# Hymba-style decoder on one core: attention logits two heads at a time, gate rows by a block diagonal, and a new place for three low parts of the output weights

## The chip, the cores and the metric

The program runs on one core of one Trainium2 chip. The metric is the device time of one execution in microseconds (us). Shorter is better. The names of the engines are those of the profile: PE does matrix products (PEld loads its weights), DVE is the vector engine, ACT the scalar engine, POOL is GpSimd, SP only issues DMAs.

## What is computed

The reference is a decoder of two layers over 1024 tokens of width 1024. Each layer projects the normed input once, gives the parts to three mixers, maps their outputs by one output projection, and adds a SwiGLU feed-forward block:

```python
h = rms_norm(x, norm_w[0])
proj = h @ w_in
(mq, mk, mv, mo, mi, mf, aq, ak, av, iq, ik, iw, sz, sxbc, sdt) = jnp.split(proj, _split_points(), axis=-1)
hm = mlstm_chunkwise(...)        # 4 heads of 64, exponential gates
ha = dsa_attention(...)          # 4 heads of 64, each query keeps its 256 best keys by an indexer
hs = ssd_mixer(...)              # 8 heads of 64, state 128, causal convolution, gate
mix = jnp.concatenate([hm, ha, hs], axis=-1) @ w_out
x = x + rms_norm(mix, norm_w[1])
h = rms_norm(x, norm_w[2])
ff = (jax.nn.silu(h @ w_gate) * (h @ w_up)) @ w_down
x = x + rms_norm(ff, norm_w[3])
```

In the attention every query block of 128 tokens sees the keys up to its own end, keeps those that the indexer chose, and takes a softmax over `q·k / 8`.

## The kernel before

A layer has three stages. **Stage a** (0 to 489 us in layer 0) makes the projection in 29 units of 128 output columns. A unit is 48 products of 128x512 (line L915): each float32 operand is split in a high and a low part, and three of the four products are taken. Between the units stand the indexer, the top-k search (VectorE), the gates of the recurrent mixers, and the attention. **Stage b** (489 to about 640 us) runs the two recurrent mixers over 8 chunks `c` of 128 tokens and then the output projection `mix` (L1853), whose weights are split into `wohi` (ScalarE, L1965) and `wolo` (`w_out_lo`: GpSimd L1683, or VectorE). **Stage e** is the feed-forward block, about 640 us. Layer 1 repeats all of it (its attention ends at 1832 us, its stage b begins at 1844 us).

Nothing schedules the work at run time: each engine has one queue, whose order is the order of the calls in the code, and semaphores (`Signal`) order the engines among each other.

**The attention** is 32 steps `m` in each layer: query block `c = m // 4` and head `h = m % 4`, over `(c + 1) * 128` keys. Steps 0 to 7 stand two at a time in projection units 21 to 24, steps 8 to 31 stand one after each eighth of units 26 to 28 (an eighth is six L915 products), and a tail follows. For step `k` PE issues `values(k-4)` (L1073), `turn_weights(k-2)` (L1062, transposes of the exponentials) and the logits of step `k`. For query blocks 0 to 3 the logits of two heads are made together at each even step (`two_logits`, L1053), one head into each PSUM bank; a head has 64 rows of the PE array to itself. For blocks 4 to 7 one head at a time is made (`logits`, L1043), 512 keys into one bank and the rest into the next. VectorE then adds the mask and takes the row maximum (`maximum`, L1284, into the tile `lg`) and scales it to the exponent's offset (L1288); ScalarE runs for step `k` first `turned_out(k-2)` (L775, copy of the transposes to `pt`) and then `exps(k)` (L767). `turn_weights(m)` waits for `exps(m)` and for `turned_out(m-1)`.

**The gate columns** (`gate_columns`, L955 to L963): small float32 products that spread values of one partition over all 128, after projection unit 6. VectorE's search waits for them.

**Stage b on GpSimd** (`b_gpsimd`) is for each chunk: `wk` (L1690), `xw` (L1694), a wait for PE's last use of the old `xdt` (L1839), `xdt` (L1697), `smem` (L1701), and the skip product (L1704); `w_out_lo` stands behind the skip product of some chunks. VectorE's queue of a chunk ends with a normalisation: L2073 (`catr`, which PE's L1775 turns), later L2131, L2134, L2136, L2137, L2138 (`nd`), whose square ScalarE takes (L1915) before its weight work (L1965 or L1955) and the next chunk's exponentials `pm` (L1905).

Of the kernel before, what the change touches and what calls it, by code (L numbers as in the profile page):

```python
# [30 lines left out]
P = 128  # L31
# [84 lines left out]
def build(nc, x, positions, norm_w, w_in, gate_b, m_norm_w, conv_w, conv_b, dt_bias, a_log, d_skip, s_norm_w,  # L116
# [6 lines left out]
    with ctx:  # L123
# [185 lines left out]
        rows_v = sig("rows_v", 12)  # L309
# [147 lines left out]
        def layer(L):  # L457
# [42 lines left out]
            lg, pt, oatt = [iq[:, 0], iq[:, 1]], [ik[:, :], smw[:, :, :].rearrange("p k n -> p (k n)")], [cosf[:, 0:AH * HD], cosf[:, AH * HD:2 * AH * HD]]  # L500
            mx, nb, sm_, rs = 32, 36, 40, 48
            N_PAIRS = NT * AH
            pair23 = ps[:, 2:4, :].rearrange("p a b -> p (a b)")
# [4 lines left out]
            c_qk = sig("c_qk", N_PAIRS)  # L508
            c_max = sig("c_max", N_PAIRS)
# [10 lines left out]
            dots = lambda m: pair23 if m >= 4 * AH else ps[:, 2 + m % 2, :]  # L520
# [151 lines left out]
            def a_scalar(act):  # L672
# [89 lines left out]
                def exps(m):  # L762
                    c, h = divmod(m, AH)
                    act.wait_ge(*c_bias(L, m + 1))
                    if h == 0 and c >= 2:
                        act.wait_ge(*c_out(L, 2 * (c - 2) + 1))
                    act.activation(lg[m % 2][:, 0:width[c]], lg[m % 2][:, 0:width[c]], ACT.Exp,  # L767
                                   bias=small[:, nb + m % 2:nb + m % 2 + 1], scale=HD ** -0.5,
                                   accum_out=small[:, sm_ + AH * (c % 2) + h:sm_ + AH * (c % 2) + h + 1]).then_inc(c_exp.sem, 1)
# [41 lines left out]
                def gate_decays():  # L811
                    s, n, bank = aux("mcol")
                    act.wait_ge(*rows_v(L, 12))
# [85 lines left out]
            def a_tensor(pe):  # L899
# [132 lines left out]
                def logits(m):  # L1032
                    c, h = divmod(m, AH)
                    q = slice(HD * (h % 2), HD * (h % 2) + HD)
                    if m == 0:
                        pe.wait_ge(*copied(aux_names[-1]))
                        pe.wait_ge(*copied(aux_names[-2]))
                    elif m >= 2:
                        pe.wait_ge(*c_max(L, m if c >= 4 else m - 1))
                    dst = dots(m)  # L1040
                    for b0 in range(0, width[c], HALF):
                        b1 = min(b0 + HALF, width[c])
                        mm = pe.matmul(dst[:, b0:b1], aq[q, h // 2, c * P:(c + 1) * P], ak[q, h // 2, b0:b1],  # L1043
                                       start=True, stop=True)
                    mm.then_inc(c_qk.sem, 1)

                def two_logits(m):

                    c, h = divmod(m, AH)
                    pe.wait_ge(*c_max(L, m))  # L1050
                    for i in range(2):
                        q = slice(HD * i, HD * i + HD)
                        pe.matmul(dots(m + i)[:, 0:width[c]], aq[q, h // 2, c * P:(c + 1) * P], ak[q, h // 2, 0:width[c]],  # L1053
                                  start=True, stop=True).then_inc(c_qk.sem, 1)

                def turn_weights(m):
# [4 lines left out]
                    for j in range(c + 1):  # L1061
                        mm = pe.transpose(ps[:, 4 + j // 4, (j % 4) * P:(j % 4 + 1) * P], lg[m % 2][:, j * P:(j + 1) * P], ident[:, :])  # L1062
# [64 lines left out]
            def a_vector(v):  # L1127
# [92 lines left out]

                def gate_decays():
# [25 lines left out]
                gate_maxima()  # L1247

# [27 lines left out]
                def maximum(m):  # L1276
                    c, h = divmod(m, AH)
                    if h == 0 and c >= 2:
                        v.wait_ge(*selected(L, c - 1))
                    v.wait_ge(*c_qk(L, m + 1))  # L1280
                    if m >= 2:
                        v.wait_ge(*c_turn(L, m - 1))
                    v.memset(small[:, 61:62], 0.0)
                    v.tensor_tensor_reduce(lg[m % 2][:, 0:width[c]], dots(m)[:, 0:width[c]],  # L1284
                                           score[:, sbase[c]:sbase[c] + width[c]], 1.0, -3.4e38, ALU.add, ALU.max,
                                           small[:, mx + m % 2:mx + m % 2 + 1]).then_inc(c_max.sem, 1)
                    v.wait_ge(*c_max(L, m + 1))
                    v.tensor_scalar(small[:, nb + m % 2:nb + m % 2 + 1], small[:, mx + m % 2:mx + m % 2 + 1],  # L1288
                                    -(HD ** -0.5), None, ALU.mult).then_inc(c_bias.sem, 1)
# [16 lines left out]
                def attend(m):  # L1306

                    maximum(m)
# [365 lines left out]
            def b_gpsimd(pool):  # L1674
# [10 lines left out]
                for c in range(NT):  # L1685
# [8 lines left out]
                    pool.tensor_tensor(xw[:, :, :], x_rows(c), gate_of(scol, c, 2, SH, HD), ALU.mult).then_inc(xw_in.sem, 1)  # L1694
                    if c:
# [10 lines left out]
                    if c in (2, 3, 7):  # L1706
                        w_out_lo({2: 0, 3: 1, 7: 2}[c])
# [1016 lines left out]
```

## Time and profile before

| | |
|---|---|
| runs before, us | 2733.35, 2733.85, 2742.17 (median 2733.85) |
| profiled execution, us | 2733.39, its span 2731.5 |
| PE busy share of the span | 96% |
| mean granted TensorE clock | 0.98 |

The span goes from the first to the last instruction of the profile; the 1.9 us around it belong to the execution. Busy shares are averages over stages, so what a part is worth is read from its own stage.

### The profile page before, as it was taken

Reading aid. Unit: us, or ns where it says so; the run is one execution under the profiler, and the core shown is the slowest. Engines: PE = TensorE matmul, PEld = TensorE weight load, DVE = VectorE, ACT = ScalarE, POOL = GpSimd, SP = SyncE. Lnnn points to the kernel's source line nnn. Section 1 sums busy time; section 2 is a strip of 40 time slices with the busy share of each in tenths; the row PEclk is TensorE's granted clock in tenths of the full one; section 3 lists DMA queues with packets and bytes.
Section 4 is the critical chain, followed back from the end, with each engine's and each line's share of the span. In section 5 each row is a group of like instructions: output and inputs, shape, how many; then the busy total and the mean of one; then the engine's idle time right before and its main releaser. Section 6 shows DMA issues by size and latency. Waiting matters only on the chain. (4 is left out here: it accounts for less than half of the span.)

```text
span 2731.5 us, 35727 instructions
## 1 busy us (share of the span) xinstructions
PE 2619.0 (96%) x12716; PEld 2123.4 (78%) x12716; DVE 1824.6 (67%) x2888; ACT 1096.3 (40%) x2074; POOL 1231.3 (45%) x776
## 2 busy tenths in 40 slices
PE   6999999899799999999989999999998999999997
PEld 5678877778688888888766888777786888888886
DVE  5579964673866666666665899547747666666666
ACT  4336434674422223232343363347644223233223
POOL 1348310431655445665433582104227445665545
PEclk8999999999999999999999999999999999999999
DMA  4213310622111111111431133106221111111113
GB/s 139 54 35 93 116 64 9 187 90 93 39 62 62 47 46 46 61 46 61 136 97 37 51 93 113 52 18 195 95 78 62 47 47 47 61 46 61 61 46 131
DMA packets 185793, 199.82 MB, mean 73 GB/s; under 512 B 17680, under 2 KB 161168, under 8 KB 185664
## 3 DMA queue, kind: packets, MB, share of 16 engines
q1 hardware_dynamic: 179904, 177.15, 20.9%
q10 hardware_dynamic: 5760, 20.97, 2.0%
q8 instruction: 77, 1.26, 0.2%
q14 instruction: 52, 0.43, 0.0%
HBM read 157.08 MB, written 38.80 MB: 72 GB/s over the span
## 5 line engine op out<-in xcount | busy, mean ns | idle before, releaser
L2269 POOL TENSOR_TENSOR ring_lo<-ring_sum,ring_hi 128x512 fp32r<-128x512 f32 x200 | 306.3, 1548 | 474.3 <-ACT ring_hi L2357 474.3
L2491 PE MATMUL ps<-form_hi,ring_hi 128*128 128x512 f32 x1232 | 484.4, 393 | 23.9 <-POOL ring_lo L1522 19.8
L2491 PE MATMUL ps<-form_lo,ring_hi 128*128 128x512 f32 x1232 | 482.7, 392 | 0.0
L2491 PE MATMUL ps<-form_hi,ring_lo 128*128 128x512 f32 x1232 | 482.5, 392 | 0.0
L915 PE MATMUL ps<-act_hi,whi 128*128 128x512 f32 x928 | 377.6, 407 | 8.5 <-ACT smr L429 8.4
L2579 DVE TENSOR_TENSOR yacc<-yacc,ps 128x1024 f32<-128x1024 f32 x176 | 214.8, 1221 | 243.6 <-PE ps L2517 243.6
L2357 ACT ACTIVATE ring_hi<-ring_sum 128x512 fp32r<-128x512 f32 x200 | 125.3, 633 | 625.9 <-DVE ring_sum L2567 625.7
L915 PE MATMUL ps<-act_hi,wlo 128*128 128x512 f32 x928 | 366.0, 394 | 0.0
L915 PE MATMUL ps<-act_lo,whi 128*128 128x512 f32 x928 | 365.9, 394 | 0.0
L1326 DVE TENSOR_SCALAR_CACHE_REDUCE ties<-score,kth 128x384 uint8<-128x384 f32 (+5 forms) x396 | 348.4, 942 | 4.8
L621 POOL TENSOR_TENSOR wlo<-raw,whi 128x1024 fp32r<-128x1024 f32 x54 | 132.2, 2448 | 410.2 <-ACT whi L676 410.2
L2491 PEld LDWEIGHTS ps<-form_hi,ring_hi 128*128 128x128 f32 x1232 | 233.4, 189 | 76.8 <-POOL ring_lo L1522 13.7
L2517 PE MATMUL ps<-ring_hi,hhi 128*128 128x512 f32 x704 | 276.0, 392 | 1.1 <-POOL hlo L2280 0.6
L2517 PE MATMUL ps<-ring_lo,hhi 128*128 128x512 f32 x704 | 275.0, 391 | 0.0
L2517 PE MATMUL ps<-ring_hi,hlo 128*128 128x512 f32 x704 | 274.9, 390 | 0.0
L2491 PEld LDWEIGHTS ps<-form_hi,ring_lo 128*128 128x128 f32 x1232 | 233.3, 189 | 49.0
L2491 PEld LDWEIGHTS ps<-form_lo,ring_hi 128*128 128x128 f32 x1232 | 233.5, 189 | 48.3
L915 PEld LDWEIGHTS ps<-act_hi,whi 128*128 128x128 f32 x928 | 176.9, 191 | 70.8 <-issue 29.9
L1568 DVE TENSOR_TENSOR gate_t<-gate_t,ps 128x512 f32<-128x512 f32 x176 | 116.9, 685 | 168.2 <-PE ps L2491 168.2
L2567 DVE TENSOR_TENSOR ring_sum<-ff_raw 128x512 f32<-128x512 f32 x200 | 210.5, 1077 | 4.8 <-DMA ff_raw<-in_w_gate 4.6
L915 PEld LDWEIGHTS ps<-act_hi,wlo 128*128 128x128 f32 x928 | 176.7, 190 | 38.4
L915 PEld LDWEIGHTS ps<-act_lo,whi 128*128 128x128 f32 x928 | 177.1, 191 | 33.7
(319 smaller groups left out, 4619.2 us busy)
## 6 DMA issues: line engine op xcount, KB each, us to landing
raw<-in_w_in SPq DMA_DIRECT2D x56, 512.0 KB, 3.9
ff_raw<-in_w_gate SPq DMA_DIRECT2D x22, 1024.0 KB, 5.4
ff_raw<-in_w_up SPq DMA_DIRECT2D x22, 1024.0 KB, 5.3
ff_raw<-in_w_down SPq DMA_DIRECT2D x22, 1024.0 KB, 4.9
proj_scratch<-stage ACTq DMA_DIRECT2D x40, 512.0 KB, 2.7
wc<-proj_scratch SPq DMA_DIRECT2D x14, 1280.0 KB, 6.7
xmid_scratch<-xres SPq DMA_DIRECT2D x16, 512.0 KB, 2.6
resid<-xmid_scratch SPq DMA_DIRECT2D x16, 512.0 KB, 6.9
```

The costliest lines, as they stand in the source:

```text
L621: pool.tensor_tensor(wlo[u % 2][:, :], raw[u % 2][:, :], whi[u % 2][:, :].bitcast(F32), ALU.subtract)\
L915: mm = pe.matmul(ps[:, half, :], w[:, k], a[half][:, k, :], start=(k == 0 and m == 0), stop=(k == KT - 1 and m == 2))
L1326: v.tensor_scalar(tie(c), of(c), at(kth, c), 0.0, op, ALU.add, accum_out=at(held, c))
L1568: v.tensor_tensor(q, q, src, op).then_inc(m_drain.sem, 1)
L2269: pool.tensor_tensor(flat_form(ring_lo[slot]), src, flat_form(ring_hi[slot]).bitcast(F32), ALU.subtract)\
L2357: act.activation(flat_form(ring_hi[slot]), src, ACT.Copy).then_inc(f_hi.sem, 1)
L2491: mm = pe.matmul(ps[:, product_bank(r, i), :], w[:, k], a[:, k], start=(k == 0 and m == 0), stop=(k == 3 and m == 2))
L2517: mm = pe.matmul(place(t)[:, cols], h[:, j, rows], w, start=(j == 0 and m == 0), stop=(j == 1 and m == 2))
L2567: v.tensor_tensor(flat_form(ring_sum[slot]), weight_part(ff_raw[place[0]], *a), weight_part(ff_raw[place[0]], *b), op)\
L2579: v.tensor_tensor(yacc[t][:, :], yacc[t][:, :], place(t), ALU.add).then_inc(y_add.sem, 1)
```

## The change

Three parts.

1. For query blocks 4 to 7 the logits are made for two heads at a time: the even step makes the first 512 keys of both heads (`two_logits(m, 0)`), the odd step the rest of both (`two_logits(m, 1)`). Each head has a bank of its own. The exponentials get four buffers `lg` in place of two (the two new ones are `nrow0`, `nrow1`), VectorE takes a maximum for each part, and both offsets (`bias`) are made in the odd step. In every step the logits now stand before `turn_weights`.
2. In `gate_columns` the 4 products of L957 and the 8 of L960 become two, with a matrix of ones and a block diagonal that VectorE makes earlier (`gate_ends`: one memset and two products).
3. `w_out_lo` 0, 1 and 2 stand on GpSimd between `xw` and `xdt` of chunks 3, 4 and 7; they stood behind the skip product of chunks 2, 3 and 7.

```diff
+            ones_rows = work[0:SH, 192:320]
+            m_ends = work[0:MH, 0:64].rearrange("p (h w) -> p h w", w=2 * NT)
+            s_ends = work[0:SH, 64:128].rearrange("p (h c) -> p h c", c=NT)
...
-            lg, pt, oatt = [iq[:, 0], iq[:, 1]], ...
+            lg, pt, oatt = [iq[:, 0], iq[:, 1], nrow[0][:, :], nrow[1][:, :]], ...
...
-                    pe.wait_ge(*copied("arow"))
+                    pe.wait_ge(*rows_v(L, 12))
                     for c in range(NT):
                         pe.matmul(bank[:, MH * c:MH * (c + 1)], mrow[0:MH, c * P:(c + 1) * P], ident[0:MH, 0:MH], start=True, stop=True)
-                    for h in range(MH):
-                        pe.matmul(bank[:, 32 + 16 * h:48 + 16 * h], const(K_SEL + P * h, P)[0:MH], mpl,
-                                  start=True, stop=True)
-                    for h in range(SH):
-                        pe.matmul(bank[:, 96 + 8 * h:104 + 8 * h], const(K_SEL + P * h, P)[0:SH],
-                                  arow[0:SH, P - 1::P], start=True, stop=True)
+                    pe.matmul(bank[:, 32:96], ones_rows[0:MH], work[0:MH, 0:64], start=True, stop=True)
+                    pe.matmul(bank[:, 96:160], ones_rows, work[0:SH, 64:128], start=True, stop=True)
...
+                def two_logits(m, part):
                     c, h = divmod(m, AH)
...
+                    else:
+                        pe.wait_ge(*c_max(L, dots_before(m, part)))
+                    cols = part_of(c, part)
                     for i in range(2):
                         q = slice(HD * i, HD * i + HD)
-                        pe.matmul(dots(m + i)[:, 0:width[c]], aq[q, h // 2, c * P:(c + 1) * P], ak[q, h // 2, 0:width[c]],
+                        pe.matmul(dots(m + i)[:, 0:cols.stop - cols.start], aq[q, h // 2, c * P:(c + 1) * P], ak[q, h // 2, cols],
                                   start=True, stop=True).then_inc(c_qk.sem, 1)
...
                     if k >= 4:
                         values(k - 4)
+                    if k < N_PAIRS and k % 2 == 0:
+                        two_logits(k, 0)
+                    elif ONE_PART <= k < N_PAIRS:
+                        two_logits(k - 1, 1)
                     if 2 <= k < N_PAIRS + 2:
                         turn_weights(k - 2)
-                    if k < 4 * AH:
-                        if k % 2 == 0:
-                            two_logits(k)
-                    elif k < N_PAIRS:
-                        logits(k)
...
+                def gate_ends():
+                    own = lambda n, w: ident[0:n, 0:n].rearrange("p (h o) -> p h o", o=1).broadcast_to([n, n, w])
+                    v.memset(ones_rows, 1.0)
+                    v.tensor_tensor(m_ends, mpl.rearrange("p (o w) -> p o w", o=1).broadcast_to([MH, MH, 2 * NT]), own(MH, 2 * NT), ALU.mult)
+                    v.wait_ge(*copied("arow"))
+                    then(v.tensor_tensor(s_ends, arow[0:SH, P - 1::P].rearrange("p (o c) -> p o c", o=1).broadcast_to([SH, SH, NT]),
+                                         own(SH, NT), ALU.mult))
...
-                    maximum(m)
+                    if m < ONE_PART:
+                        maximum(m, 0)
+                        bias(m)
+                    elif m % 2 == 0:
+                        maximum(m, 0)
+                        maximum(m + 1, 0)
+                    else:
+                        for i in (m - 1, m):
+                            maximum(i, 1)
+                            bias(i)
...
                     pool.tensor_tensor(xw[:, :, :], x_rows(c), gate_of(scol, c, 2, SH, HD), ALU.mult).then_inc(xw_in.sem, 1)
+                    if c in (3, 4, 7):
+                        w_out_lo({3: 0, 4: 1, 7: 2}[c])
...
-                    if c in (2, 3, 7):
-                        w_out_lo({2: 0, 3: 1, 7: 2}[c])
```

On PE, in the last query block (c = 7) of layer 1, the queue of before reads as follows. A row is a line of the kernel, the operation, its output and inputs, the output's shape and how often it stands in a row; `ik` and `smw` are the two `pt` buffers, `iq` and `nrow` the `lg` buffers.

```order
L1073 MATMUL ps<-avr,smw 128x64 x7
L1062 MATMUL ps<-ident,iq 128x128 x7
L1043 MATMUL ps<-ak,aq 128x512 x2
L915 MATMUL ps<-act_hi1,whi0 128x512
L915 MATMUL ps<-act_lo1,whi0 128x512
L915 MATMUL ps<-act_hi1,wlo0 128x512
L915 MATMUL ps<-act_hi1,whi0 128x512
L915 MATMUL ps<-act_lo1,whi0 128x512
L915 MATMUL ps<-act_hi1,wlo0 128x512
L1073 MATMUL ps<-avr,ik 128x64 x7
L1062 MATMUL ps<-ident,iq 128x128 x8
L1043 MATMUL ps<-ak,aq 128x512 x2
```

The same place of the changed kernel (L1052 are the logits there, L1061 the transposes, L928 the projection):

```order
L1072 MATMUL ps<-avr,smw 128x64 x7
L1052 MATMUL ps<-ak,aq 128x512 x2
L1061 MATMUL ps<-ident,nrow1 128x128 x7
L928 MATMUL ps<-act_hi1,whi0 128x512
L928 MATMUL ps<-act_lo1,whi0 128x512
L928 MATMUL ps<-act_hi1,wlo0 128x512
L928 MATMUL ps<-act_hi1,whi0 128x512
L928 MATMUL ps<-act_lo1,whi0 128x512
L928 MATMUL ps<-act_hi1,wlo0 128x512
L1072 MATMUL ps<-avr,ik 128x64 x7
L1052 MATMUL ps<-ak,aq 128x512 x2
L1061 MATMUL ps<-ident,iq 128x128 x8
```

The number of products is the same: the pair of logits is now one product of each of two heads instead of two products of one head, and it has moved ahead of the transposes.

On GpSimd, in chunks 2 to 4 of layer 0's stage b, before (from the skip product of chunk 2; `wolo2` and `wolo3` are the first two low parts):

```order
L1704 TENSOR_TENSOR rw0<-rw0,dskip 128x512
L1683 TENSOR_TENSOR wolo2<-raw0,wohi2 128x1024
L1690 TENSOR_TENSOR wk<-rw1,gcol 128x256
L1694 TENSOR_TENSOR xw<-rw1,scol 128x512
L1697 TENSOR_TENSOR xdt<-rw1,scol 128x512
L1701 TENSOR_TENSOR smem<-smem,decs 128x512
L1704 TENSOR_TENSOR rw1<-rw1,dskip 128x512
L1683 TENSOR_TENSOR wolo3<-raw1,wohi3 128x1024
L1690 TENSOR_TENSOR wk<-rw0,gcol 128x256
```

And now, from the same product on:

```order
L1730 TENSOR_TENSOR rw0<-rw0,dskip 128x512
L1714 TENSOR_TENSOR wk<-rw1,gcol 128x256
L1718 TENSOR_TENSOR xw<-rw1,scol 128x512
L1707 TENSOR_TENSOR wolo2<-raw0,wohi2 128x1024
L1723 TENSOR_TENSOR xdt<-rw1,scol 128x512
L1727 TENSOR_TENSOR smem<-smem,decs 128x512
L1730 TENSOR_TENSOR rw1<-rw1,dskip 128x512
L1714 TENSOR_TENSOR wk<-rw0,gcol 128x256
L1718 TENSOR_TENSOR xw<-rw0,scol 128x512
L1707 TENSOR_TENSOR wolo3<-raw1,wohi3 128x1024
L1723 TENSOR_TENSOR xdt<-rw0,scol 128x512
```

Both low parts have moved from behind a skip product to behind the next chunk's `xw`, where `xdt`, `smem` and the skip product of that chunk now stand behind them.

## Rows read from the trace of the kernel before

**Rows 1.** Windows, layer 0's late attention: us, PE, PEld, DVE, ACT, POOL busy, clock, DMA.

```profile
376.00:478.00 102.00, 102.00 (x566) 75.26 (x564) 52.40 (x129) 43.94 (x82) 4.65 (x2) 1.00 0.06 22
```

**Rows 2.** PEld timeline, blocks 4 and 7: start, us, instruction [idle before, releaser].

```profile
408.08 0.29 PEld L1043 LDWEIGHTS ps<-ak,aq 64*128 64x128 f32 x2 [0.17 <-issue]
...
409.36 0.19 PEld L915 LDWEIGHTS ps<-act_hi,whi 128*128 128x128 f32 x1
...
463.90 0.29 PEld L1043 LDWEIGHTS ps<-ak,aq 64*128 64x128 f32 x2 [0.17 <-issue]
...
465.81 0.19 PEld L915 LDWEIGHTS ps<-act_hi,whi 128*128 128x128 f32 x1 [0.76 <-issue]
...
469.80 0.29 PEld L1043 LDWEIGHTS ps<-ak,aq 64*128 64x128 f32 x2 [0.17 <-issue]
```

**Rows 3.** PEld timeline, two heads together, 128 keys and then 512.

```profile
314.81 0.30 PEld L1053 LDWEIGHTS ps<-ak,aq 64*128 64x128 f32 x4 [0.35 <-issue]
315.23 0.19 PEld L915 LDWEIGHTS ps<-act_hi,whi 128*128 128x128 f32 x1
...
393.16 0.30 PEld L1053 LDWEIGHTS ps<-ak,aq 64*128 64x128 f32 x4 [0.17 <-issue]
394.22 0.19 PEld L915 LDWEIGHTS ps<-act_hi,whi 128*128 128x128 f32 x1 [0.76 <-issue]
```

**Rows 4.** Timeline of VectorE and ScalarE, one step of block 7.

```profile
465.93 1.22 DVE L1284 CUSTOM_DVE_ANT_0 iq<-ps,score 128x1024 f32<-128x1024 f32 x1 [4.41 <-issue]
...
467.38 1.15 ACT L767 ACTIVATE iq<-iq,small 128x1024 f32<-128x1024 f32 x1 [2.46 <-DVE small L1288]
...
469.91 1.02 ACT L775 ACTIVATE ik<-ps 128x1024 f32<-128x1024 f32 x1 [1.02 <-PE ps L1062]
```

**Rows 5.** PEld timeline, gate columns of layer 0, then of layer 1.

```profile
153.66 1.82 PEld L957 LDWEIGHTS ps<-ties,cst 4*128 4x128 f32 x8
155.37 3.53 PEld L960 LDWEIGHTS ps<-arow,cst 8*128 8x128 f32 x16
158.78 0.97 PEld L963 LDWEIGHTS ps<-small,cst 4*128 4x128 f32 x4
...
1509.38 0.97 PEld L957 LDWEIGHTS ps<-ties,cst 4*128 4x128 f32 x8
...
1512.64 0.97 PEld L963 LDWEIGHTS ps<-small,cst 4*128 4x128 f32 x4
```

**Rows 6.** Window over layer 0's gate columns, columns as in rows 1.

```profile
153.00:160.00 7.00, 7.00 (x34) 6.98 (x34) 0.21 (x3) 0.16 (x1) 2.29 (x1) 0.50 0.29 77
```

**Rows 7.** One line's durations (ns, least/median/most): L2134 in both layers.

```profile
L2134 DVE SCALAR_TENSOR_TENSOR small<-nd x16: 165/166/2341, 503.0 to 1943.1; 128x4 f32<-128x4 f32 x16
```

**Rows 8.** Timeline of all engines, end of chunk 2 (layer 0).

```profile
521.47 2.35 POOL L1683 TENSOR_TENSOR wolo<-raw,wohi 128x1024 fp32r<-128x1024 f32 x1
...
521.57 2.54 DVE L2073 TENSOR_TENSOR catr<-nd,small 128x256 f32<-128x256 f32 x1
...
524.25 0.30 PE L1775 MATMUL ps<-ident,catr 128*128 128x128 f32 x1 [2.33 <-DVE catr L2073]
```

**Rows 9.** Timeline of all engines, `xw` and normalisation around chunks 3 and 4.

```profile
525.09 1.04 POOL L1694 TENSOR_TENSOR xw<-rw,scol 128x512 f32<-128x512 f32 x1
...
528.63 0.17 DVE L2134 SCALAR_TENSOR_TENSOR small<-nd 128x4 f32<-128x4 f32 x1
...
539.59 1.04 POOL L1694 TENSOR_TENSOR xw<-rw,scol 128x512 f32<-128x512 f32 x1
...
540.87 0.17 DVE L2134 SCALAR_TENSOR_TENSOR small<-nd 128x4 f32<-128x4 f32 x1
...
542.61 0.42 ACT L1915 ACTIVATE hsq<-nd 128x256 f32<-128x256 f32 x1 [2.13 <-DVE nd L2138]
```

**Rows 10.** Timeline of all engines, chunk 7.

```profile
578.41 1.04 ACT L1965 ACTIVATE wohi<-wo_raw 128x1024 fp32r<-128x1024 f32 x1
...
579.86 0.69 DVE L2145 TENSOR_TENSOR y<-y,rw 128x512 f32<-128x512 f32 x1
```

More of the change, by code:

```diff
@@ L308, in build @@
         aux_free = [sig(f"aux_free{s}", (n_aux + 1 - s) // 2) for s in range(2)]
-        rows_v = sig("rows_v", 12)
+        rows_v = sig("rows_v", 13)
         rows_a = sig("rows_a", 5)
@@ L507, in layer @@
             c_clear = sig("c_clear", 4)
-            c_qk = sig("c_qk", N_PAIRS)
-            c_max = sig("c_max", N_PAIRS)
+            c_qk = sig("c_qk", N_DOTS)
+            c_max = sig("c_max", N_DOTS)
             c_bias = sig("c_bias", N_PAIRS)
@@ L519, in layer, with dots_before, part_of @@
             c_kept = sig("c_kept", KEPT)
-            dots = lambda m: pair23 if m >= 4 * AH else ps[:, 2 + m % 2, :]
+            dots = lambda m: ps[:, 2 + m % 2, :]
+            def dots_before(m, part=0):
+                return m if m < ONE_PART else ONE_PART + 4 * ((m - ONE_PART) // 2) + 2 * part + m % 2
+            def part_of(c, part):
+                return slice(part * HALF, min((part + 1) * HALF, width[c]))
             kept = lambda c: tiles(score[:, sbase[c]:sbase[c] + 2 * P] if c else sinf[:, HALF:HALF + 2 * P])
@@ L766, in exps @@
                         act.wait_ge(*c_out(L, 2 * (c - 2) + 1))
-                    act.activation(lg[m % 2][:, 0:width[c]], lg[m % 2][:, 0:width[c]], ACT.Exp,
-                                   bias=small[:, nb + m % 2:nb + m % 2 + 1], scale=HD ** -0.5,
+                    act.activation(lg[m % 4][:, 0:width[c]], lg[m % 4][:, 0:width[c]], ACT.Exp,
+                                   bias=small[:, nb + m % 4:nb + m % 4 + 1], scale=HD ** -0.5,
                                    accum_out=small[:, sm_ + AH * (c % 2) + h:sm_ + AH * (c % 2) + h + 1]).then_inc(c_exp.sem, 1)
@@ L812, in gate_decays @@
                     s, n, bank = aux("mcol")
-                    act.wait_ge(*rows_v(L, 12))
+                    act.wait_ge(*rows_v(L, 13))
                     act.activation(scol[:, :, 2, :], scol[:, :, 2, :], ACT.Exp).then_inc(rows_a.sem, 1)
@@ L1037, in logits @@
                         pe.wait_ge(*copied(aux_names[-2]))
[L1038 to L1050, printed above, removed]
+                    else:
+                        pe.wait_ge(*c_max(L, dots_before(m, part)))
+                    cols = part_of(c, part)
                     for i in range(2):
                         q = slice(HD * i, HD * i + HD)
-                        pe.matmul(dots(m + i)[:, 0:width[c]], aq[q, h // 2, c * P:(c + 1) * P], ak[q, h // 2, 0:width[c]],
+                        pe.matmul(dots(m + i)[:, 0:cols.stop - cols.start], aq[q, h // 2, c * P:(c + 1) * P], ak[q, h // 2, cols],
                                   start=True, stop=True).then_inc(c_qk.sem, 1)
@@ L1247, in a_vector @@
                 gate_maxima()
+                gate_ends()
                 v.wait_ge(*copied("iw"))
@@ L1274, in a_vector, with maximum, bias @@
                 v.wait_ge(*c_clear(L, 4))
-                def maximum(m):
+                def maximum(m, part):
                     c, h = divmod(m, AH)
-                    if h == 0 and c >= 2:
+                    n = dots_before(m, part) + 1
+                    cols = part_of(c, part)
+                    if h == 0 and part == 0 and c >= 2:
                         v.wait_ge(*selected(L, c - 1))
[L1280 to L1289, printed above, removed]
+                    v.wait_ge(*c_qk(L, n))
+                    if m >= 4 and part == 0:
+                        v.wait_ge(*c_turn(L, m - 3))
+                    v.memset(small[:, clear + 2 * part + m % 2:clear + 2 * part + m % 2 + 1], 0.0)
+                    v.tensor_tensor_reduce(lg[m % 4][:, cols], dots(m)[:, 0:cols.stop - cols.start],
+                                           score[:, sbase[c] + cols.start:sbase[c] + cols.stop], 1.0, -3.4e38, ALU.add, ALU.max,
+                                           small[:, mx + 4 * part + m % 4:mx + 4 * part + m % 4 + 1]).then_inc(c_max.sem, 1)
+                def bias(m):
+                    first, second, to = [small[:, k:k + 1] for k in (mx + m % 4, mx + 4 + m % 4, nb + m % 4)]
+                    if m < ONE_PART:
+                        v.wait_ge(*c_max(L, dots_before(m) + 1))
+                        v.tensor_scalar(to, first, -(HD ** -0.5), None, ALU.mult).then_inc(c_bias.sem, 1)
+                    else:
+                        v.wait_ge(*c_max(L, dots_before(m, 1) + 1))
+                        v.tensor_scalar(to, first, second, -(HD ** -0.5), ALU.max, ALU.mult).then_inc(c_bias.sem, 1)
                 def rows_out(c):
@@ L1306, in attend @@
                 def attend(m):
-                    maximum(m)
+                    if m < ONE_PART:
+                        maximum(m, 0)
[3 more added lines that the diff above has]
+                        maximum(m + 1, 0)
+                    else:
+                        for i in (m - 1, m):
+                            maximum(i, 1)
+                            bias(i)
                     if m % AH == 3 and m >= 7:
```

11 lines of the change are left out of this document (5 added, 6 removed).

## Prediction

> **What bounds the kernel now.** I read the windows of the three stages first, then the waits of each engine in those stages, then the timelines around the edited lines. In the late attention (units 26 to 28) PE is busy in all 102 us of the window at full clock, while VectorE works 52.40 us, ScalarE 43.94 and GpSimd 4.65 [rows 1]. Layer 1 shows the same stage again. So in this stretch what PE no longer has to do comes off the time, as long as the other two keep up. The gate columns are a piece of PE's queue too, with nothing beside it: VectorE is busy 0.21 us of 7 there, since its search waits for the result [rows 6]. Stage b is another matter. There a chain runs once round PE, VectorE and ScalarE for each chunk, and a delay of one link is a delay of all that follows. The feed-forward stage is not touched; a shift that reaches it is kept.
>
> **Logits, the term of the sum.** Before, one head of query block 4 takes PE from 408.08 to the next product's weights at 409.36, 1.28 us; one of block 7 takes 463.90 to 465.81, 1.91 us [rows 2]. The blocks between lie on the line of these two, 0.21 us for each 128 keys: 1.49 and 1.70. Two heads together, one in each half of the array, take 0.42 us for 128 keys and 1.06 us for 512 [rows 3], so 0.63 and 0.84 for 256 and 384. In other words two heads cost what one costs. A pair of heads is now 512 keys of both and then the rest of both: 1.06 + 0.42 = 1.48 us in block 4 where 2 x 1.28 = 2.56 stood, a gain of 1.08. Block 5: 2.98 - 1.69 = 1.29; block 6: 3.40 - 1.90 = 1.50; block 7: 3.82 - 2.12 = 1.70. The four make 5.57 us, and each block has two pairs: 11.1 us per layer. Each step has as many changes between half-height and full-height products as it had, so the idle stretch that goes with them [0.17 and 0.76 us in rows 2 and 3] is in both prices.
>
> What must stay hidden is the chain behind the odd step, because both offsets now wait for the second part. Count from the end of the second part in block 7. VectorE needs some 0.85 us to the first offset (half of the 1.22 us of the 1024-wide maximum is 0.61, plus fixed cost; I take 0.7 and 0.15), ScalarE 1.15 and about 0.2 for the exponential, then 1.02 for the copy of the transposes [rows 4]: with hand-overs 3.4 us. PE asks for both at `turn_weights` one step later. A step was 5.90 us (463.90 to 469.80, rows 2) and is now 5.90 - 1.91 + 1.06 = 5.05. That leaves 1.65 us of slack. The second exponential is wanted a step later still. In the smaller blocks step and chain shrink together. Only in the tail, where no projection stands between the steps, is the copy late: after the last logits PE has about 2 us of its own work before the 3.4 us are over. I charge 1.0 us per layer (0.5 to 1.5), so **10.1 us per layer, 20.2 in all**.
>
> **Gate columns.** L957 is 8 passes and L960 is 16 (two passes for each float32 product). In layer 0 the 24 take 153.66 to 158.78, 5.12 us, or 0.21 each; the granted clock is 0.50 there, the lower of the two levels (1.2 GHz). In layer 1 they take 1509.38 to 1512.64, 3.26 us, because the first of them still run at the full 2.4 GHz [rows 5, 6]. Passes of 16 columns and of 8 cost the same, so the number of passes sets the price, and the new products are 4. At 0.21 us that is 0.85, at layer 1's 0.12 (0.97 / 8) it is 0.5. A 64-column pass is not in these rows; if it were twice as long, 0.9 us of the gain would go in each layer. I take 4.3 us for layer 0 and 2.7 for layer 1, **7.0 us**. If the clock's way back up depends on when the products began to be small, the units behind stay slow for longer and half of it (3.5 us) is lost. The three VectorE instructions of `gate_ends` are small, stand well ahead of their use, and are covered by VectorE's waits for ScalarE and PE there; uncovered they would cost about 1 us in each layer.
>
> **The low parts.** GpSimd and VectorE disturb each other. L2134 works on 4 numbers per partition and takes 166 ns, but in one chunk of each layer 2341 [rows 7]: there a `w_out_lo` runs. In chunk 2 L2073 starts 0.10 us behind a `w_out_lo` and takes 2.54 us, its whole length, and PE waits 2.33 for it [rows 8]. This collision of before goes away: 2.3 us gained per layer.
>
> The new places have collisions of their own. `xw` of chunk 3 ends at 526.13. L2134 of that chunk ran at 528.63 with PE 2.33 us late; without that it is due at 526.3, so 0.2 us into the new `w_out_lo` [rows 8, 9]. It waits about 2.2 us, L2136 and L2138 wait behind it, and `xdt`, due at once, gets in between. Gain and loss of chunks 2 and 3 cancel. In chunk 4 `xw` ends at 540.63 and L2134 comes at 540.87, again into the new `w_out_lo`; ScalarE has been waiting 2.13 us for the end of this very chain (L2138) and goes on to the next exponentials [rows 9]. So chunk 4 loses 2.3 us. In chunk 7 the low part waits for ScalarE's `wohi`, ready at 579.45, and L2145 starts 0.4 us later [rows 10]: it and the next two-input operations wait, the part of it that VectorE's waits for ScalarE absorb is 0.5 to 1.2, and 1.4 to 2.2 us come out at the start of `mix`. The sum is a **loss of 4 us per layer, 8 in all**; the bounds are a gain of 4.6 in all (nothing collides at the new places) and a loss of 14 (all three new ones cost their 2.35 and the 2.3 of chunk 2 are not regained).
>
> The Trainium skill, GPSIMD Engine Reference, section Key points, says that GpSimd shares its SBUF interfaces with VectorE and that they contend when VectorE's instruction has two SBUF inputs or runs in a two-port mode. By that rule L2134, L2136, L2138 and L2145 are the ones to be stopped, and an idle stretch of GpSimd is no free place. The trace agrees for L2073 and L2134. Without the rule the low parts would fill idle time, and the sum would be the first rival's 2701.6.
>
> **The sum.** The profiled execution is 2733.4 us, span 2731.5 and 1.9 around it. 2733.4 - 20.2 - 7.0 + 8.0 = 2714.2. The median of the runs lies 0.5 above the profiled one. I say **2714** for the median.
>
> **Rivals.**
> *The low parts fit.* GpSimd is idle between `xw` and `xdt`, and VectorE's two-input operations might come early or late enough. Then 2.3 us per layer are gained and nothing lost: 2733.4 - 20.2 - 7.0 - 4.6 = 2701.6. Against it: the two starts in rows 9 lie 0.2 us behind `xw`, and a `w_out_lo` is 2.35 long.
> *The chain behind the odd step takes back half of the logits.* A step of the top-k search in VectorE's queue ahead of the second maxima would do it: 0.6 us of wait beyond the slack for each of 16 pairs is 10 us, which gives 2724. For it: two offsets and both exponentials bunch up in one step. Against it: VectorE is idle for half of the window.
> *It doesn't do what it says.* The two heads' products don't overlap when they alternate between first and second part, or the step is set by VectorE and ScalarE: logits 0, gate 7 gained, low parts 8 lost: 2734, no change. Against it: rows 3 are the same instruction with 512 keys.
> *Slower.* One mechanism: `turn_weights` in the odd-to-even step waits for the second part's exponential and the copy that is queued behind it. The place is PE's L1061 of the changed kernel. Without it 19.2 us are left as gain, so it decides from 1.2 us of wait for each of 16 pairs on, which is a chain 2.85 us longer than the 3.4 counted. At 2 us of wait each (a chain of 7.05 us) the time is 2714.2 + 32 = 2746. For it: before, the offset came after each head and no copy stood behind it. Against it: ScalarE is busy 43.94 of 102 us.
>
> **Numbers.** Within 0.3% (8 us) a measurement of this kernel can't be told from no change. The forecast (2708 to 2719, from tail, gate clock and collisions) has 0.62, the low parts that fit (2698 to 2707) 0.15, half of the logits (2719 to 2725) 0.12, no change 0.07, slower 0.04. The first three are faster by more than 0.3%: 0.89; same 0.07, slower 0.04. The range of 2699 to 2724 holds these three but for their ends.
>
> **What would show it.** Right: the pairs of logits at 1.06 and 0.42 to 1.06 us; the window of the late attention still full of PE work and 10 us shorter in both layers; the gate columns 2.5 to 4.5 us shorter; L2134 of chunks 3 and 4 at over 2 us behind L1707 of the changed kernel, L2145 of chunk 7 likewise, and stage b 4 us longer. Wrong: waits on PE at L1061 for ScalarE; steps of block 7 at 5.9 us still; short L2134 in chunks 3 and 4; a window at half clock behind the gate columns that is longer than before. The greatest weakness is the order in which VectorE and GpSimd get their turns within 0.3 us in chunks 3 and 4: a shift of the chain of that size moves the collision to another operation, or away.

## The result, and the profile after

The changed kernel takes 2713.96 us (median of 5 runs, 2707.98 to 2715.47) against 2733.85 before: a ratio of 0.9917 with a 95% interval of 0.9896 to 0.9937. The profiled execution took 2715.47 us with a span of 2713.3, that is 18.2 us less span than before. The forecast was 2714, so the total fits; its terms fit less well, and they made up for each other. That the two agree to the microsecond is luck, also because the five runs of the changed kernel alone lie 7.5 us apart.

**The late attention** is still all PE work at full clock. These are its windows in both layers (columns as in [rows 1]):

```profile
373.00:459.00 86.00, 86.00 (x541) 68.05 (x540) 53.41 (x170) 39.57 (x79) 3.65 (x2) 1.00 0.06 21
1716.00:1802.00 86.00, 86.00 (x541) 68.04 (x540) 53.65 (x171) 39.58 (x79) 3.84 (x2) 1.00 0.06 22
```

From the turn of the first finished query block to the last logits it took 98.71 us before and takes 86.68 now in layer 0, and 98.70 and 86.67 in layer 1: 12.0 us less. The weight loads of PE show the pair of one odd step of block 7 at the price that [rows 3] gave, 454.70 to 455.76 = 1.06 us, and the transposes directly behind it:

```profile
449.84 0.30 PEld L1052 LDWEIGHTS ps<-ak,aq 64*128 64x128 f32 x4
450.90 0.75 PEld L1061 LDWEIGHTS ps<-ident,nrow 128*128 128x128 f32 x7 [0.76 <-issue]
...
452.88 1.76 PEld L1072 LDWEIGHTS ps<-avr,ik 128*128 128x128 f32 x14
454.70 0.30 PEld L1052 LDWEIGHTS ps<-ak,aq 64*128 64x128 f32 x4
455.76 0.85 PEld L1061 LDWEIGHTS ps<-ident,iq 128*128 128x128 f32 x8 [0.76 <-ACT iq L780]
456.59 0.19 PEld L928 LDWEIGHTS ps<-act_hi,whi 128*128 128x128 f32 x1
```

The only new wait of the attention's steps is in the tail, where PE's transposes of head 30 wait for ScalarE's copy, as the prediction said (PE timeline):

```profile
464.12 1.06 PE L1061 MATMUL ps<-ident,nrow 128*128 128x128 f32 x8 [0.55 <-ACT smw L788]
```

The tail, from the last logits to the last turn, is 0.71 us longer (12.14 to 12.85). Three things make that up: the last logits themselves are 0.85 us shorter, the transposes of head 29, which stood ahead of them, now come behind (0.92), and the wait adds about 0.6. Window and tail together, the logits are worth 11.3 us per layer.

**The gate columns**: the two new products take 153.41 to 154.26 in layer 0 and 1497.48 to 1497.93 in layer 1 (weight loads of PE; the rows answer to [rows 5]):

```profile
153.41 0.54 PEld L969 LDWEIGHTS ps<-ties 4*128 4x128 f32 x2
153.84 0.54 PEld L970 LDWEIGHTS ps<-ties 8*128 8x128 f32 x2
154.26 0.97 PEld L972 LDWEIGHTS ps<-small,cst 4*128 4x128 f32 x4
...
1497.48 0.30 PEld L969 LDWEIGHTS ps<-ties 4*128 4x128 f32 x2
1497.71 0.30 PEld L970 LDWEIGHTS ps<-ties 8*128 8x128 f32 x2
1497.93 0.52 PEld L972 LDWEIGHTS ps<-small,cst 4*128 4x128 f32 x4
```

From the first gate column to the next projection product it was 8.25 us and 6.03 before, and is 4.52 and 2.77: 3.7 and 3.3 us less, 7.0 together.

**The low parts** run into VectorE at all three new places. The timelines of GpSimd and VectorE show them side by side, chunks 3, 4 and 7 of layer 0:

```profile
514.07 2.35 POOL L1707 TENSOR_TENSOR wolo<-raw,wohi 128x1024 fp32r<-128x1024 f32 x1
...
527.35 2.34 POOL L1707 TENSOR_TENSOR wolo<-raw,wohi 128x1024 fp32r<-128x1024 f32 x1
...
568.34 2.51 POOL L1707 TENSOR_TENSOR wolo<-wo_raw,wohi 128x1024 fp32r<-128x1024 f32 x1 [2.39 <-ACT wohi L1989]
```

```profile
513.99 0.17 DVE L2158 SCALAR_TENSOR_TENSOR small<-nd 128x4 f32<-128x4 f32 x1
514.19 2.24 DVE L2160 TENSOR_TENSOR small<-small,gcol 128x4 f32<-128x4 f32 x1
...
527.63 2.08 DVE L2158 SCALAR_TENSOR_TENSOR small<-nd 128x4 f32<-128x4 f32 x1
529.75 0.96 DVE L2160 TENSOR_TENSOR small<-small,gcol 128x4 f32<-128x4 f32 x1
...
568.67 2.72 DVE L2169 TENSOR_TENSOR y<-y,rw 128x512 f32<-128x512 f32 x1
```

L2158, L2160 and L2169 are L2134, L2136 and L2145 of before. Operations on 4 numbers per partition take over 2 us when a low part runs beside them. In chunk 3 it is L2160 that is caught: L2158 started 0.08 us ahead of the low part and kept its 0.17 us.

**What the sum did not have** is the start of stage b. There PE's granted clock is at the lower level (1.2 GHz) for a while in both kernels, but now for longer. The windows of the kernel before, and of the changed one, from the start of the stage:

```profile
490.00:494.00 4.00, 3.19 (x15) 2.27 (x16) 0.00 (x0) 2.79 (x5) 1.70 (x3) 0.60 0.90 259
494.00:498.00 4.00, 4.00 (x46) 3.10 (x45) 0.75 (x2) 2.03 (x9) 1.19 (x2) 0.97 0.92 261
```

```profile
475.00:479.00 4.00, 3.37 (x16) 2.31 (x17) 0.00 (x0) 2.49 (x5) 1.97 (x3) 0.60 0.98 270
479.00:483.00 4.00, 4.00 (x35) 2.73 (x33) 0.00 (x0) 1.01 (x4) 0.65 (x1) 0.50 1.19 290
483.00:487.00 4.00, 4.00 (x21) 3.70 (x20) 2.94 (x6) 2.24 (x10) 0.43 (x1) 0.62 1.09 360
```

To the exponentials of chunk 1 it took 15.49 us in layer 0 and 16.14 in layer 1; in this execution it takes 18.77 and 19.81, 7.0 us more in all.

The account of the span, before to after, in us: logits -22.6; gate columns -7.0, of which 1.4 comes back ahead of the late attention, 0.7 in each layer; collisions of the low parts +4.7; start of stage b +7.0; two more stretches of half clock in layer 1's stage b, behind the new collisions of chunks 4 and 7, +2.7; the rest -4.4. That is -18.2 (-22.6 - 7.0 + 1.4 + 4.7 + 7.0 + 2.7 - 4.4). Half of the rest, 2.2 us, lies between layer 0's output projection and layer 1's gate columns, where nothing was changed; what makes it is not shown.

In stage b the chunks are best read by the starts of ScalarE's first exponential of each chunk (L1905 of before). Four differences carry what is said below, each for layer 0 / layer 1, in us, all worked out from the timelines of the runs (one profiled execution of each kernel):

| kernel | stage start to chunk 1 | chunk 2 to 3 | 3 to 4 | 7 to `mix` |
|---|---|---|---|---|
| before | 15.49 / 16.14 | 14.21 / 14.22 | 13.06 / 13.06 | 8.61 / 8.61 |
| after | 18.77 / 19.81 | 13.28 / 13.28 | 14.82 / 14.83 | 10.13 / 11.22 |
| e1_logits | 19.64 / 19.78 | 16.44 / 16.30 | 14.98 / 14.11 | 8.62 / 8.61 |
| e2_gate | 15.71 / 15.80 | 13.41 / 14.22 | 17.64 / 13.06 | 8.61 / 8.61 |
| e3_low_parts | 15.70 / 16.14 | 13.28 / 13.28 | 14.83 / 14.83 | 11.03 / 10.15 |
| e4_no_low_move | 19.02 / 19.61 | 14.22 / 14.22 | 13.06 / 13.06 | 8.61 / 8.60 |
| e5_behind_catr | 16.12 / 19.78 | 10.80 / 10.80 | 13.05 / 13.06 | 9.54 / 8.61 |
| e6_tail_filled | 18.73 / 14.79 | 10.80 / 10.81 | 13.06 / 13.06 | 8.61 / 8.61 |
| e7_start_filled | 15.28 / 14.73 | 10.80 / 10.79 | 13.04 / 13.06 | 8.61 / 8.60 |
| e8_logits_behind | 15.60 / 18.78 | 17.60 / 14.22 | 14.42 / 13.05 | 8.61 / 8.61 |
| e9_both_filled | 14.79 / 16.46 | 10.80 / 10.79 | 13.05 / 13.06 | 8.60 / 8.60 |
| e10_catr_only | 16.34 / 19.00 | 10.81 / 10.81 | 13.05 / 13.06 | 8.61 / 8.60 |

### The profile page after: what moved, and what is told of

Read it like the earlier page. It is cut to its first block and busy times, and to the rows that moved or that the text cites. A ratio compares the mean times of both kernels' runs of the same rounds, so it can differ in the third digit from the quotient of the medians.

```text
span 2713.3 us, 35747 instructions
## 1 busy us (share of the span) xinstructions
PE 2596.4 (96%) x12676; PEld 2111.4 (78%) x12676; DVE 1842.0 (68%) x2990; ACT 1090.3 (40%) x2074; POOL 1235.6 (46%) x776
## 5 line engine op out<-in xcount | busy, mean ns | idle before, releaser
L928 PE MATMUL ps<-act_hi,whi 128*128 128x512 f32 x928 | 376.6, 406 | 9.6 <-ACT smr L429 8.4
L928 PE MATMUL ps<-act_hi,wlo 128*128 128x512 f32 x928 | 365.5, 394 | 0.0
L928 PE MATMUL ps<-act_lo,whi 128*128 128x512 f32 x928 | 364.9, 393 | 0.0
L928 PEld LDWEIGHTS ps<-act_hi,whi 128*128 128x128 f32 x928 | 176.6, 190 | 58.5 <-issue 19.0
L928 PEld LDWEIGHTS ps<-act_hi,wlo 128*128 128x128 f32 x928 | 176.3, 190 | 38.4
L928 PEld LDWEIGHTS ps<-act_lo,whi 128*128 128x128 f32 x928 | 177.1, 191 | 33.7
```

The source lines that it names most:

```text
L928: mm = pe.matmul(ps[:, half, :], w[:, k], a[half][:, k, :], start=(k == 0 and m == 0), stop=(k == KT - 1 and m == 2))
```

## The experiments

The first four take the change apart.

**e1_logits**: only part 1.

```diff
 # the kernel before, with
+ two_logits(m, part), four lg buffers, maximum(m, part), bias(m), logits ahead of turn_weights
 # gate_columns and the places of w_out_lo as before
```

> Only the logits, two heads at a time; gate columns and low parts as before. The account of the prediction: 10.1 us less in each layer's late attention, so 2733.9 - 20.2 = 2713.7. The profile of the full change showed half clock for 3.3 to 3.7 us longer at the start of each stage b. If the new tail of the attention causes it, it shows here too and the time is 2717 to 2720. Rival, that the gain is mostly in other parts: above 2725.

2720.2 us, ratio 0.9955 (0.9939 to 0.997), some 12 us. The late attention is 86.67 us in both layers, as in the full change, and the tail 12.85. So the logits themselves give their 11.3 us per layer. In the profiled execution stage b takes 15.1 of these 22.6 us away: its start is 4.2 and 3.6 us longer, and behind the old collision in chunk 2 the clock stays low for longer than in the profile of before, 4.1 and 3.1 us over chunks 2 to 4. The span is 13.2 us shorter all the same, since it gains 5.7 us in places that the change does not touch. The window 516 to 526 us, behind the collision of chunk 2 in layer 0 (PE fully busy at half clock):

```profile
516.00:526.00 10.00, 10.00 (x62) 8.44 (x61) 6.26 (x15) 5.15 (x15) 1.04 (x1) 0.50 0.63 184
```

**e2_gate**: only part 2.

```diff
 # the kernel before, with
+ two products with ones_rows in gate_columns, gate_ends() on VectorE
```

> Only the gate columns by two products and a block diagonal. The account: 4.3 us less in layer 0 and 2.7 in layer 1, so 2726.9. Rival, that the way back to the full clock takes half of it: 2730.4. Start of stage b as before, if the attention's tail is what lengthens its half clock.

2727.88 us, ratio 0.9979 (0.9967 to 0.999), 2.7 to 9 us: the forecast 7.0 lies in that, and so does the rival's 3.5. The rows decide: the gate columns are 4.49 and 2.77 us long, 3.8 and 3.3 less than before. The start of stage b is as before. The chunks of layer 0 are not, though nothing was changed there: chunk 3 to 4 and 4 to 5 take 17.64 and 14.14 us (13.06 and 11.74 before), at a granted clock of 0.50 from 533.4 to 550.3. From the first attention step to the first turn it takes 63.07 us in layer 0 where it took 62.17; PE's waits in that stretch show where most of the 0.9 us comes from. PE waits 0.8 us for ScalarE's copies of the projection out of PSUM, and there is no such wait in the kernel before; why ScalarE is late is not shown:

```profile
PE ps L918 <- ACT stage L705: 0.8, 2, 0.5
```

**e3_low_parts**: only part 3.

```diff
 # the kernel before, with
+                    if c in (3, 4, 7):            # between xw and xdt
+                        w_out_lo({3: 0, 4: 1, 7: 2}[c])
-                    if c in (2, 3, 7):            # behind the skip product
-                        w_out_lo({2: 0, 3: 1, 7: 2}[c])
```

> Only the three low parts between xw and xdt. The account: the collision of chunk 2 goes, those of chunks 3, 4 and 7 come, 2.3 to 4 us more in each stage b, so 2739 to 2742. Rival, that the low parts fit into GpSimd's idle time: 4.6 us less, 2729. The sign decides.

2739.39 us, ratio 1.0023 (1.001 to 1.0035): slower by 2.7 to 9.6 us. The sign is the account's. The steps are those of the full change: chunk 2 to 3 is 0.93 us shorter than before, 3 to 4 is 1.77 longer, 7 to `mix` 1.54 to 2.42. VectorE's two operations of 4 numbers again take the length of what GpSimd does beside them:

```profile
526.72 2.24 DVE L2136 TENSOR_TENSOR small<-small,gcol 128x4 f32<-128x4 f32 x1
...
540.15 2.09 DVE L2134 SCALAR_TENSOR_TENSOR small<-nd 128x4 f32<-128x4 f32 x1
```

**e4_no_low_move**: parts 1 and 2.

```diff
 # the changed kernel, with w_out_lo behind the skip products of chunks 2, 3 and 7
-                    if c in (3, 4, 7):
-                        w_out_lo({3: 0, 4: 1, 7: 2}[c])
+                    if c in (2, 3, 7):
+                        w_out_lo({2: 0, 3: 1, 7: 2}[c])
```

> Logits and gate columns changed, low parts as before. The account: 5 to 8 us faster than the full change, 2706 to 2709, with L2073's collision of 2.5 us in chunk 2 back and the short L2134 in chunks 3 and 4. Rival, that the new places are the better ones: 2718.

2709.47 us by the median, but its ratio of 0.9916 (0.9895 to 0.9938) can't be told from the 0.9917 of the full change. Only the steps of the table agree with the account: 14.22, 13.06 and 8.60 where the full change has 13.28, 14.83 and 10.13. It does not decide; e3 does.

By their ratios the three parts alone come to -12, -6 and +6 us, -12 together, beside -23 for the full change. The intervals (8 to 17 less, 3 to 9 less, 3 to 10 more, and 17 to 28 less) are too wide to say that the parts don't add up. In the profiled executions e1 lost 7.3 us behind chunk 2, both layers together, and e2 6.1 us in layer 0's stage b, both at half clock and in chunks that neither of them changes.

**e5_behind_catr**: a place for the low parts that the table suggests. VectorE's L2073 has two SBUF inputs; of what follows it up to L2134 nearly every operation reads PSUM, and beside GpSimd those kept their own length in the timelines read here (0.41 us for 128x260, 0.68 for 128x512). So the low part goes behind L2073.

```diff
 # e4_no_low_move, with
                     if c in (2, 3, 7):
+                        pool.wait_ge(*m_out(L, c))
                         w_out_lo({2: 0, 3: 1, 7: 2}[c])
```

> Logits and gate columns changed; the low parts behind the skip products of chunks 2, 3 and 7 as in the kernel before, but each waits first for L2073 of its chunk. If the collision with L2073 is the whole price of the old place: the step from chunk 2 to 3 falls from 14.2 to 11.9 us, nothing else in stage b moves, and the time is some 5 us below that of the version with the old place, 2704 to 2706 beside 2709.5. Rival, that the low part only moves its collision to L2134: no gain.

2694.95 us, ratio 0.9848 (0.983 to 0.9865): faster than both kernels. The step from chunk 2 to 3 is 10.80 us in both layers, so the old collision cost 3.4 us, not 2.3. That is 6.8 us for both layers together, but the ratio is some 18 us below that of e4_no_low_move (8 to 30 by the ends of the intervals), and the 2704 to 2706 that were expected were missed by 9 us. What gives the rest is not shown: the profiled execution (2702.50) was the slowest of five, and the other four (2693.13 to 2695.07) have no profile. Now the low part starts right behind L2073 and ends before the next `wk`; VectorE's row of the same time keeps its 0.68 us:

```profile
508.15 2.36 POOL L1707 TENSOR_TENSOR wolo<-raw,wohi 128x1024 fp32r<-128x1024 f32 x1 [0.54 <-DVE catr L2098]
510.60 0.61 POOL L1714 TENSOR_TENSOR wk<-rw,gcol 128x256 f32<-128x256 f32 x1
```

```profile
508.32 0.68 DVE L2137 TENSOR_TENSOR y<-ps,scol 128x512 f32<-128x512 f32 x1
...
512.10 0.17 DVE L2159 SCALAR_TENSOR_TENSOR small<-nd 128x4 f32<-128x4 f32 x1
512.30 0.16 DVE L2161 TENSOR_TENSOR small<-small,gcol 128x4 f32<-128x4 f32 x1
```

**e10_catr_only**: the same wait in the kernel before, and nothing else.

```diff
 # the kernel before, with
                     if c in (2, 3, 7):
+                        pool.wait_ge(*m_out(L, c))
                         w_out_lo({2: 0, 3: 1, 7: 2}[c])
```

> The kernel before with one wait more: the three low parts wait for L2073 of their chunk. If the collision of chunk 2 costs what the step from chunk 2 to 3 shows (14.2 before, 10.8 without it), each layer gains 3.4 us and the time is 2734 - 7 = 2727 (ratio 0.9975), and more where the half clock behind the stall would have lasted longer. Rival, that the gain came only together with the changed attention: no change.

2726.48 us, ratio 0.9976 (0.9967 to 0.9985), chunk 2 to 3 again 10.81 us. One wait gains as much as the gate columns do.

**e8_logits_behind**: the order within a step.

```diff
 # e4_no_low_move, with, in attend(k)
+                    if 2 <= k < N_PAIRS + 2:
+                        turn_weights(k - 2)
                     if k < N_PAIRS and k % 2 == 0:
                         two_logits(k, 0)
                     elif ONE_PART <= k < N_PAIRS:
                         two_logits(k - 1, 1)
-                    if 2 <= k < N_PAIRS + 2:
-                        turn_weights(k - 2)
```

> Logits and gate columns changed, low parts as before, but in each step the logits stand behind turn_weights as they did. The chain behind the second part (3.4 us by the prediction) then has 1.3 us of projection and 1.6 us of values before it, 2.9 us, so PE waits 0.5 us for each pair of block 7 and less in the others: late attention 1 to 4 us longer in each layer. Rival, that the chain is shorter than counted: no waits, late attention as long as with the logits ahead.

2710.46 us, ratio 0.9907 (0.989 to 0.9924): no difference in time to e4_no_low_move that can be told. The late attention and tail of layer 1 are 2.34 us longer (89.01 + 12.85 against 86.67 + 12.85), within what was expected. In layer 0 they are 5.35 us longer (89.01 + 15.86), more than was expected: behind the same wait the granted clock of PE is 0.63 and 0.52 from 464 to 468 and 468 to 472 us, and 1.00 on both sides of it. The expected mechanism is there, but small in the steps. It is largest in the tail, 1.38 us in both layers where the order of the change has 0.55 to 0.56 (PE timeline of layer 0):

```profile
464.59 1.54 PE L1061 MATMUL ps<-ident,nrow 128*128 128x128 f32 x8 [1.38 <-ACT smw L788]
```

In the steps of block 7 it shows in the weight loads of PE beside ScalarE's copy:

```profile
450.85 0.19 PEld L928 LDWEIGHTS ps<-act_hi,whi 128*128 128x128 f32 x1 [0.76 <-issue]
...
454.10 0.85 PEld L1061 LDWEIGHTS ps<-ident,iq 128*128 128x128 f32 x8 [0.22 <-issue]
455.12 0.30 PEld L1052 LDWEIGHTS ps<-ak,aq 64*128 64x128 f32 x4 [0.17 <-issue]
```

```profile
453.08 0.90 ACT L788 ACTIVATE smw<-ps 128x896 f32<-128x896 f32 x1
```

The second part of the logits ends where the projection's weights are loaded, at 450.85. The transposes start at 454.10, 3.25 us later and right behind the copy that ends at 453.98, after 0.22 us of idle time that the view puts down to "issue". The second thing to see is the 0.17 us ahead of the logits: behind the transposes they start with that idle time, behind the values with 0.07 us, too little for the view to print it (449.84 and 454.70 in the rows of the changed kernel above). So the new order saves some 0.1 us per step by itself, which the prediction had left out. With the old order layer 1 would have gained 9.0 us from the logits (98.70 + 12.14 against 89.01 + 12.85), with the new one it gains 11.3.

The last three look for the half clock at the start of stage b, all on top of e5_behind_catr.

**e6_tail_filled** fills PE's waits in the attention's tail with products that no one reads.

```diff
 # e5_behind_catr, with idle_product() = pe.matmul(ps[:, 0, :], ident, ak[:, 0, 0:512])
+                    if k == N_PAIRS:
+                        pe.wait_ge(*evicted(N_PROJ - 1, 0))
+                        idle_product()            # ahead of turn_weights(30)
...
+                idle_product()                    # ahead of the last cat_turn
```

> The version before it, with two products of 128x512 that no one reads in the attention's tail, at the two places where PE waits there (ahead of the transposes of head 30 and of the last turn). If the new waits of the tail make the half clock at the start of stage b longer, the first step of stage b goes back from 11.8 to 12.4 us to 9.85 and the time is 5 us lower, less about 1 us for the two products. Rival, that it comes from the switch of stages or from the order of the products: the first step stays at 12 us and the time is 1 us higher.

2697.9 us, ratio 0.9858 (0.984 to 0.9877). The tail is 12.87 us long, so the two products cost nothing. Layer 1 starts at full clock (14.79 us), layer 0 does not (18.73): neither the expectation nor its rival, and no gain in time.

**e7_start_filled** puts work at the start of stage b.

```diff
 # e5_behind_catr, with, at the start of b_tensor
+                for _ in range(8):
+                    pe.matmul(bank(0)[:, 0:P], ident[:, :], ident[:, :], start=True, stop=True)
```

> The version with the low parts behind L2073, with 8 small products that no one reads on PE at the start of stage b, while PE waits there for GpSimd. If the idle time at the switch of stages sets the half clock: first step back to 9.85 us, 5 us lower. If the tail before it does: no change, or half clock a little shorter, within 2 us.

2699.57 us, ratio 0.9865 (0.9847 to 0.9883). Both layers start short (15.28 and 14.73 us), but the eight products themselves run partly at half clock and make the switch of stages 2.9 and 2.5 us longer. In time nothing is gained, against the 5 us that were expected if idle time at the switch sets the clock.

**e9_both_filled** takes the tail's products and three small ones.

```diff
 # e6_tail_filled, with, at the start of b_tensor
+                for _ in range(3):
+                    pe.matmul(bank(0)[:, 0:P], ident[:, :], ident[:, :], start=True, stop=True)
```

> The version with two idle products in the attention's tail, and three small ones (in place of eight) at the start of stage b. If idle time of PE around the switch of stages sets the half clock at the start of stage b, both layers begin at full clock (first step 9.85 us) and the switch costs under 1 us: 2692 to 2695 beside 2694.95 and 2697.9. Rival, that the half clock there comes and goes whatever stands in the gaps: one layer or both with a first step of 11.8 to 12.4 us, 2695 to 2700.

2695.38 us, ratio 0.9867 (0.9852 to 0.9882), as fast as e5_behind_catr within the intervals. The switch costs nothing more (2.48 us), both layers begin at full clock, but in layer 1 the clock falls a few us later (16.46, with a first step of 11.51 where 9.85 was expected).

## Why the prediction was right

**The total** was 2714 and came out at 2714. The mechanisms of the three parts were right. The agreement of the total was luck: logits and low parts gave 2.4 and 3.3 us more than forecast, 4.4 came from places that the change leaves alone, while half clock in stage b, which the sum had at nothing, took 9.7, and 1.4 came back ahead of the attention. So the total is no proof of the terms.

**Logits.** The mechanism and the price of a pair were right: 1.06 us for two heads of 512 keys at once, no waits in the steps, 0.55 us in the tail. The term was 10.1 us per layer and measured 11.3. The 16 pairs of steps of both layers came out as counted: the logits of blocks 4 to 7 took 25.44 us per layer before and take 14.40, 11.0 less. The wait in the tail was about 0.6 us, not 1.0, and the order in the step saves idle time at the change from transposes to logits (e8), which was counted as unchanged. The chain behind the odd step was counted at 3.4 us; in the changed kernel's tail it is 3.4 (460.74 to 464.12), in the steps of e8 3.25. With 1.65 us of slack it stayed hidden, and where e8 took the slack away it began to show.

**Gate columns.** 4.3 and 2.7 us were predicted, 3.7 and 3.3 measured, 7.0 in both. The products that were replaced went as forecast, 5.12 to 0.85 us in layer 0 and 3.26 to 0.45 in layer 1. The rest is the clock: in layer 0 it fell earlier, and the columns ahead of them (L955, now L968) took 0.5 us more; in layer 1 it fell later, and those behind them (L963, now L972) took 0.5 less. That these two make up for each other is luck. The rival that the clock's way back takes half of it did not come true. 0.7 us per layer comes back ahead of the late attention, most of it in PE's waits for ScalarE's copies.

**Low parts.** The chunk and the kind of each collision were right; in chunk 3 the operation caught was L2136 and not L2134, which started 0.08 us ahead of the low part and not 0.2 behind its start, a shift of the size that the prediction named as its weakness. The Trainium skill (GPSIMD Engine Reference, section Key points) says that VectorE instructions with two SBUF inputs contend with GpSimd. The traces agree: L2134, L2136 and L2145 took 2.08, 2.24 and 2.72 us beside a low part, and operations with a PSUM input kept their 0.41 and 0.68 us. The sizes were off. Predicted were 0 for chunks 2 and 3 together, +2.3 for chunk 4 and +1.4 to 2.2 for chunk 7; measured -0.93, +1.77 and +1.52, that is 2.4 us per layer instead of 4. The first was off because the collision of before was priced by PE's wait alone (2.33 us); without it the step is 3.4 us shorter. [rows 8] shows the wait but not what follows. Layer 0 of e2 had the same collision and full clock behind it, as the windows below show, and took 13.41 us from chunk 2 to 3. So 2.6 us of the 3.4 are the stall and 0.8 the half clock behind it.

```profile
519.00:523.00 4.00, 2.87 (x26) 2.83 (x27) 3.93 (x10) 2.35 (x6) 2.31 (x3) 1.00 0.02 4
523.00:527.00 4.00, 4.00 (x50) 3.22 (x50) 3.79 (x10) 1.87 (x5) 1.04 (x1) 1.00 0.88 252
```

**Not in the sum** was the start of stage b: 7.0 us in the profiled execution. With the 2.7 us of half clock behind the new collisions of layer 1 it took what logits, low parts and the rest had given more than forecast. Without these 9.7 us the account would have come to 2704 rather than 2714.

**Rivals.** That the low parts fit is refuted by e3. That the chain takes back half of the logits is refuted by the windows of the late attention. That the pairs would not overlap is refuted by their 1.06 us. The slower rival would have needed 1.2 us of wait per pair; in the steps there is none, in the tail one of 0.55 us in each layer.

**Open.** Why the half clock at the start of stage b lasts from nothing to some 12 us. With the old logits one of eight starts was long (18.5 us or more: layer 1 of e10), with the new ones and nothing filled in eight of ten. That speaks for the new tail as a cause, but e6, which fills its waits, still has one long start of two. Of the four starts with products in the switch of stages (e7, e9) none was long, which speaks for PE's idle time there, but two kernels with one profile each don't prove it, and the times of e5, e6, e7 and e9 don't differ by more than their intervals. A part differs without any cause that the profiles show: in e8 the same stall in chunk 2 was followed by 17 us of half clock in layer 0 and by 3 in layer 1, and e2 has 17 us of it in layer 0 from 533 us on, where the kernel before has none.

## What to carry to other kernels

An idle stretch of GpSimd is a free place only if VectorE has no operation with two SBUF inputs on the path in that stretch; look for a stretch in which it reads PSUM, and order GpSimd's work there with a wait, which gained 7 us alone and, in place of part 3, came with a ratio of 0.9848. Products that use 64 rows of the array go in pairs, one in each half: two heads of 512 keys took 1.06 us, where one head of 1024 keys, the same work in two products, took 1.91. Their place in a step counts for little: behind the 64-column products they started with 0.1 us less idle time than behind the transposes, and e8's time did not show it. When a stall in front of PE is priced, add what the clock loses behind it, and don't take a sum that fits for proof of its terms.

## What was not expected of the hardware

The price of a stall on PE of about 2.3 us varied with the half clock behind it: chunk 2 to 3 and 3 to 4 took 27.3 us together in the profile of before, 31.4 in e1_logits and 32.0 in e8_logits_behind (layer 0), with the same collision in front, and 23.9 without it. Of the 8.1 us between least and most, 2.6 are the stall and 5.5 the clock.

Small float32 passes of PE cost the same at 64 columns as at 8: 0.21 us at half clock and 0.11 at full clock, in [rows 5] and in the rows of the changed kernel.
